# Expert blocks of 96 rows and twelve overflow blocks in a one-core mixture-of-experts decoder step

## What is computed

```python
logits = (xt @ w_router) + router_bias
probs = jax.nn.softmax(logits, axis=-1)
...                                   # best group of 4 experts, then the top 2 of that group
for e in range(N_EXPERTS):            # 16
    h = jax.nn.silu(xt @ w_gate[e]) * (xt @ w_up[e])      # 1024 -> 512
    y = y + gates[:, e:e + 1] * (h @ w_down[e])           # 512 -> 1024
```

## Time and profile before

| | us |
|---|---|
| median of 3 runs | 719.52 |
| lowest and highest | 718.69, 720.13 |
| the profiled execution: its time | 722.82 |
| its span in the trace | 721.0 |

### The profile page before, as it was taken

One profiled execution on the slowest core, in us unless ns is written; L12 is line 12 of the kernel. 1 busy time (PEld: TensorE's weight loads), 2 busy tenths in 40 slices (PEclk: granted clock), 3 DMA queues, 4 the chain that ended last, 5 costly groups with the idle time before them and its releaser, 6 DMA issues. The chain is left out here.

```text
span 721.0 us, 9573 instructions
## 1 busy us (share of the span) xinstructions
PE 663.5 (92%) x3807; PEld 556.4 (77%) x3807; DVE 508.0 (70%) x580; ACT 339.5 (47%) x334; POOL 125.4 (17%) x77
## 2 busy tenths in 40 slices
PE   6999999988999999999428899999999999999776
PEld 5999899988997886587417788888888888887431
DVE  4226447799575474776483899999999999998247
ACT  4437413322153421013305677777777777777100
POOL 0001323333033201200020011111111111100140
PEclk9999999999999999999559999999999999999896
DMA  9941212212512014097165799999999999990172
GB/s 285 383 167 60 78 40 88 89 59 79 156 60 76 1 49 152 21 357 271 60 223 242 283 378 410 412 415 403 408 416 411 400 410 415 410 384 37 62 275 95
DMA packets 48689, 162.56 MB, mean 225 GB/s; under 512 B 4294, under 2 KB 23450, under 8 KB 36364
## 3 DMA queue, kind: packets, MB, share of 16 engines
q1 hardware_dynamic: 41756, 136.62, 50.1%
q0 software_dynamic: 6896, 25.43, 9.0%
HBM read 142.61 MB, written 19.44 MB: 225 GB/s over the span
## 5 line engine op out<-in xcount | busy, mean ns | idle before, releaser
L1300 DVE TENSOR_TENSOR RA<-FA,RA 128x2048 fp32r<-128x2048 f32 x93 | 212.9, 2290 | 34.9 <-ACT RA L848 34.2
L848 ACT ACTIVATE RA<-FA 128x2048 fp32r<-128x2048 f32 x93 | 178.7, 1923 | 51.0 <-PE bank L1733 34.9
L1733 PE MATMUL bank<-RA 128*128 128x512 f32 x768 | 188.3, 401 | 3.7 <-DVE RA L1305 2.1
L1733 PEld LDWEIGHTS bank<-RA 128*128 128x128 f32 x768 | 143.9, 192 | 36.3 <-DVE RA L1305 2.7
L1479 PE MATMUL bank<-RA 128*128 128x272 f32 x432 | 110.4, 292 | 0.0
L1480 PE MATMUL bank<-RA 128*128 128x272 f32 x432 | 109.8, 290 | 0.0
L1745 PE MATMUL bank<-RA 128*128 128x512 f32 x384 | 91.3, 394 | 2.1 <-DVE RA L1310 2.1
L1745 PEld LDWEIGHTS bank<-RA 128*128 128x128 f32 x384 | 73.0, 190 | 17.5 <-DVE RA L1310 2.2
L1479 PEld LDWEIGHTS bank<-RA 128*128 128x128 f32 x432 | 82.5, 191 | 0.0
L1480 PEld LDWEIGHTS bank<-RA 128*128 128x128 f32 x432 | 82.5, 191 | 0.0
L969 DVE TENSOR_TENSOR RA<-FA,RA 128x2048 fp32r<-128x2048 f32 (+1 forms) x18 | 48.6, 2700 | 28.7 <-ACT RA L707 28.4
(11 more groups left out here) (223 smaller groups left out, 733.7 us busy)
## 6 DMA issues: line engine op xcount, KB each, us to landing
FA<-w_up SPq DMA_DIRECT2D x32, 1024.0 KB, 7.1
FA<-w_gate SPq DMA_DIRECT2D x32, 1024.0 KB, 6.8
FA<-w_down SPq DMA_DIRECT2D x32, 1024.0 KB, 7.6
FA<-w_in SPq DMA_DIRECT2D x13, 1024.0 KB, 5.1
y_by_slot<-FA POOLq DMA_DIRECT2D x16, 512.0 KB, 7.2
y_by_slot<-FA POOLq DMA_DIRECT2D x1, 4096.0 KB, 18.5
FA<-w_out SPq DMA_DIRECT2D x4, 1024.0 KB, 5.1
FA<-x_prompt SPq DMA_DIRECT2D x8, 256.0 KB, 5.5
```

Source lines behind the costliest of these rows:

```text
L848: nc.scalar.activation(split[split_slot(bi, j)][0], raw[place], ACT.Copy).then_inc(m_hi, 1)
L1300: tt_(sl[1], raw[place], f(sl[0]), ALU.subtract).then_inc(m_lo, 1)
L1733: last = mm(out[:, :], xgT[par][x_][:, kt, :], w[w_][:, t, :], start=(kt == 0 and i == 0), stop=(kt == KT - 1 and i == 2))
```

## The change

Blocks hold at most 96 rows (`CAP`), and there are twelve overflow blocks. Slots in DRAM stay 128 rows apart. All products, transposes, copies, gathers and stores of a block take 96 rows in place of 128; where the block's rows are partitions this shortens no instruction's free size, and where they lie along the free size it becomes 384 or 96 in place of 512 or 128. Since 96 is no power of two, DVE gets three instructions more in the routing chain, which count how often a rank passes a multiple of 96. A second fill writes zeros into rows 96 to 127 of the first 16 blocks. The fullest expert has 82 rows, so neither version runs an overflow block.

```diff
-NOV = 8
+NOV = 12
+CAP = 96
@@ routing on DVE
-            full = small[:, SM_BLK + 1:SM_BLK + NTT].unsqueeze(1).broadcast_to([P, E, 4])
-            link(tt_(more, cnt.unsqueeze(2).broadcast_to([P, E, 4]), full, ALU.is_gt))
+            limits = small[:, SM_CAP:SM_CAP + NCAP].unsqueeze(1)
+            link(tt_(more, cnt.unsqueeze(2).broadcast_to([P, E, NCAP]), limits.broadcast_to([P, E, NCAP]), ALU.is_gt))
...
             link(stt(tmp, before, -1.0, eo, ALU.add, ALU.add))
-            link(stt(t3(over), in_tile.rearrange("p (t e) -> p t e", t=NTT), float(P),
+            link(tt_(past, in_tile.unsqueeze(2).broadcast_to([P, NE, NCAP]), limits.broadcast_to([P, NE, NCAP]), ALU.is_ge))
+            link(nc.vector.tensor_reduce(pm, past, AX, ALU.add))
+            link(stt(base, pm, float(P - CAP), base, ALU.mult, ALU.add))
+            link(stt(t3(over), in_tile.rearrange("p (t e) -> p t e", t=NTT), float(CAP),
                      tmp.unsqueeze(1).broadcast_to([P, NTT, E]), ALU.is_ge, ALU.mult))
@@ one-hot rows
-                tt_(row_hot[:, sl], iota_h.unsqueeze(1).broadcast_to([P, NTT, P]),
-                    row[:, sl].unsqueeze(2).broadcast_to([P, NTT, P]), ALU.is_equal).then_inc(s_hot, 1)
+                tt_(row_hot[:, sl], iota_h[:, 0:CAP].unsqueeze(1).broadcast_to([P, NTT, CAP]),
+                    row[:, sl].unsqueeze(2).broadcast_to([P, NTT, CAP]), ALU.is_equal).then_inc(s_hot, 1)
@@ fill on POOL
             pool.dma_start(yg_dram[E * P:NBLK * P, :].rearrange("(b p) n -> p b n", p=P), fill_src).then_inc(s_fill, 16)
+            pool.dma_start(yg_dram[0:E * P, :].rearrange("(b p) n -> p b n", p=P)[CAP:P],
+                           fa(32 * K, D)[CAP:P].unsqueeze(1).broadcast_to([P - CAP, E, D])).then_inc(s_fill, 16)
@@ store on POOL
-                pool.dma_start(y_slot[bi], ysb[par]).then_inc(m_st[par], 16)
+                pool.dma_start(y_slot[bi][0:CAP], ysb[par][0:CAP]).then_inc(m_st[par], 16)
@@ low halves of a block's rows on DVE (the high halves on ACT alike)
-                    tt_(xgT[par][1][:, 4 * c:4 * c + 4, :], bank[c][:, :].rearrange("p (k t) -> p k t", k=4),
-                        f(xgT[par][0][:, 4 * c:4 * c + 4, :]), ALU.subtract).then_inc(m_tl, 1)
+                    tt_(xgT[par][1][:, 4 * c:4 * c + 4, 0:CAP], bank[c][:, 0:4 * CAP].rearrange("p (k t) -> p k t", k=4),
+                        f(xgT[par][0][:, 4 * c:4 * c + 4, 0:CAP]), ALU.subtract).then_inc(m_tl, 1)
@@ PE: the transposes of a block's rows, a gate or up product, a down product
-                        last = tr(bank[c][:, t * P:(t + 1) * P], xg[par][:, c * 512 + t:(c + 1) * 512:4], ident)
+                        last = tr(bank[c][:, t * CAP:(t + 1) * CAP], xg[par][0:CAP, c * 512 + t:(c + 1) * 512:4], ident[0:CAP, 0:CAP])
...
-                        last = mm(out[:, :], xgT[par][x_][:, kt, :], w[w_][:, t, :],
+                        last = mm(out[0:CAP, :], xgT[par][x_][:, kt, 0:CAP], w[w_][:, t, :],
...
-                            last = mm(bank[5 + g][:, :], hT[x_][:, kt, :], w[w_][:, t, 512 * g:512 * g + 512],
+                            last = mm(bank[5 + g][0:CAP, :], hT[x_][:, kt, 0:CAP], w[w_][:, t, 512 * g:512 * g + 512],
```

More of the change, by code:

```diff
@@ L197, in half @@
             return fa(off, n // 2).bitcast(BF16)
-        row_hot = half(B0, 2 * NTT * P).rearrange("p (s r) -> p s r", s=2 * NTT)
+        row_hot = half(B0, 2 * NTT * CAP).rearrange("p (s r) -> p s r", s=2 * NTT)
         off_blk = fa(B0 + 1024, 2 * NTT * NBLK).rearrange("p (s b) -> p s b", s=2 * NTT)
@@ L626, in gather @@
                 pool.indirect_dma_start(
-                    out=xg[par], out_offset=None, in_=x1_dram,
-                    in_offset=bass.IndirectOffsetOnAxis(ap=ids[:, bi:bi + 1].bitcast(U32), axis=0)).then_inc(m_xg[par], 16)
+                    out=xg[par][0:CAP], out_offset=None, in_=x1_dram,
+                    in_offset=bass.IndirectOffsetOnAxis(ap=ids[0:CAP, bi:bi + 1].bitcast(U32), axis=0)).then_inc(m_xg[par], 16)
             pool.wait_ge(s_x1s, 16 * NTT)
@@ L864, in silu @@
                     act.wait_ge(m_h, bi)
-                nc.scalar.activation(silu_g, bank[2][:, :], ACT.Silu).then_inc(m_sg, 1)
+                nc.scalar.activation(silu_g[0:CAP], bank[2][0:CAP, :], ACT.Silu).then_inc(m_sg, 1)
             def y_half(bi, par):
@@ L870, in y_half @@
                     act.wait_ge(m_st[par], store_count(bi, par))
-                nc.scalar.activation(ysb[par][:, 0:512], bank[5][:, :], ACT.Copy).then_inc(m_ya, 1)
+                nc.scalar.activation(ysb[par][0:CAP, 0:512], bank[5][0:CAP, :], ACT.Copy).then_inc(m_ya, 1)
             def step(bi, par, s=None, i=0):
@@ L1190, in _ @@
             base, nb, before, over = rb(360, NE), rb(440, 32), rb(472, E), rb(504, NE)
-            more = rb(664, 4 * E).rearrange("p (e j) -> p e j", e=E)
-            rank, tmp = rb(264, NE), rb(728, E)
+            more = rb(664, NCAP * E).rearrange("p (e j) -> p e j", e=E)
+            rank, tmp = rb(264, NE), rb(760, E)
+            past = fa(B0 + 1024, NE * NCAP).rearrange("p (x j) -> p x j", j=NCAP)
             prod = fa(B0 + 1024, 2 * NE)
@@ L1710, in _ @@
                     for w in range(2):
-                        last = mm(bank[5][:, 0:NBLK], row_hot[0:rows, i, :], in_blk[0:rows, i, w, :],
+                        last = mm(bank[5][0:CAP, 0:NBLK], row_hot[0:rows, i, :], in_blk[0:rows, i, w, :],
                                   start=(i == 0 and w == 0), stop=(i == 2 * NTT - 1 and w == 1))
@@ L1754, in h_turn @@
                     c, t = kt // 2, kt % 2
-                    last = tr(bank[4][:, kt * P:(kt + 1) * P], hbuf[:, c * 256 + t:(c + 1) * 256:2], ident)
+                    last = tr(bank[4][:, kt * CAP:(kt + 1) * CAP], hbuf[0:CAP, c * 256 + t:(c + 1) * 256:2], ident[0:CAP, 0:CAP])
                 last.then_inc(m_ht, 1)
```

26 lines of the change are left out of this document (14 added, 12 removed).

## The result

| | before | after |
|---|---|---|
| median (4 runs each) | 719.83 us | 731.14 us |
| ratio | | 1.0129, 95% interval 1.0099 to 1.0159 |
| the profiled execution's span | 721.0 | 730.9 |

The change makes the kernel 1.3% slower, about 9 us, by the ratio with its interval. (The two medians of four lie further apart, 11.3 us.) Repeated beside other runs of the kernel before (median 722.4), it was 1.0095 (1.0063 to 1.0126), about 7 us. The forecast was 721.1 with a range of 716.0 to 723.3: the sign was right, and the size was far off.

What follows compares the result with a forecast made beforehand. PE, nine tenths busy or more in nearly every slice, was taken as the bound. Terms +1.3 + 1.05 - 0.27 - 0.1 (steady stretch) - 0.35 = +1.6 us gave 721.1; range 716.0 to 723.3, the forecast's own 719.2 to 722.9.

Steps and rivals of the forecast that it cites:

- Routing, +1.3 us: Serial DVE chain until `ids`: three new steps and more blocks, less shorter one-hot rows, +1.3 us, between +0.9 and +1.9.
- The table, +1.05: Overflow table on DVE: four more pairs take 1.65 us, 0.6 of it covered; exposed +1.05 us, between 0.6 and 1.65.
- `x_lo`, -0.27: Low half before the first product, for which PE waits: two instructions go from 1.29 to 1.02 us, -0.27.
- A: Rival, faster: the moving identity sets the transposes' pace, so narrowing it saves 5.2 us, giving 715.9; chance 0.13.
- B: Rival, no difference: transposes lose their stride penalty, or table and chain end low with 1 us from the clock; 719.1; chance 0.25.
- C: Rival, slower: the second fill from 32 partitions runs slowly and delays the `w_in` piece; 721.5 to 730; chance 0.06.
- D: Rival: an expert with more than 96 rows would run an overflow block of 17.9 us; fullest has 82, so none.
- Products, 0: Expert products on PE: 96 instead of 128 stationary columns buys nothing, 0, bounded by -0.3 us.
- transposes, 0: Transposes on PE: the stationary side of 128 strided columns sets 0.120 us a step and is unchanged, so 0.
- the transposes' half of B: Transposes on PE lose only their penalty for the stride, 0.012 us each over 172, 2.1 us.
- The tail, -0.35: After the last expert: shorter `h_lo` and a smaller last store before the final gathers, -0.35 us, between 0 and -0.8.
- The fill, 0: Second fill adds 10.5 us ahead of the `w_in` piece, landing at about 48, before ACT's use at 52.94: hidden, 0.

Runs made afterwards that it cites:

- after_cast_128: The changed kernel with one edit: DVE copies the index list on 128 partitions again instead of 96; 725.55 us, ratio 1.0044 to the kernel before.
- after_tokens_128: The changed kernel with one-hot rows and index products back at 128 columns and the index copy on 128 partitions; ratio 1.0026 to the kernel before.

## Why the prediction was wrong

The direction has a reason and isn't luck: without the slow gather the changed kernel is still slower, by the two terms of the sum that were positive. The size failed, by one wait. The working, step by step:

- **Routing, +1.3 us: +1.84.** The DVE terms were right. 1.33 and the 0.53 us of the second ten index products give 1.86. The missing term is PE's, which stood nowhere in my list: I had taken a narrower stationary operand as free, from products of 512 moving columns, and these have 28. The copy itself comes 2.79 us later; 0.95 of that stands ahead of the chain.
- **The table, +1.05, and `x_lo`, -0.27: the step that failed.** "The gather and the transposes move with `ids`, so the cover stays." The gather did not move with `ids`: it came 6.6 us late, 4.4 on POOL and 2.2 that go with the weights issued ahead, and the first product came 5.8 us later after the copy, not 0.8. The wait had been taken as fixed; it grew from one low half to three. Where the copy is on 128 partitions, in after_cast_128 and after_tokens_128, the distance is 13.6 and 13.7 us against 12.8 to 13.0, +0.6 to +0.9: there the sum of the two terms, +0.78, holds. The time, too, by and large: 1.0044 and 1.0026, +3.2 and +1.9 us, where the sum said +1.6 and with PE's term 2.1.
- **The warning** stood in the trace of the kernel before: its first two gathers, beside the low halves, take 2.26 and 1.82 us and its third 0.94 (the rows above). Had I asked what they waited for, a longer wait would have been a rival. None of A, B, C and D held it.
- **Products, 0, and transposes, 0: right.** 288.1 us from first to last gate product in both; eight transposes 1.10 us after 1.12, so rival A and the transposes' half of B are out. The four of the hidden rows end 0.10 us sooner (0.60 after 0.70), and 24 down products take 0.07 more (5.68 after 5.61), which cancel. The prediction's "whatever the stride" is my reading of the Trainium skill ("TensorE: Matmul & The Clock Gate", the section on LDWEIGHTS), whose formula names the columns alone; no row here bears it out, and strided transposes follow each other at 0.120 us where contiguous ones do at 0.108.
- **The tail, -0.35: right in part.** From the last store to the first of the final gathers it is 5.03 us, before 5.21, -0.18; over all profiles it is 4.97 to 5.04 with stores of 96 rows and 5.02 to 5.33 with 128. The span after the start of the last gate product is 1.3 us longer in the first profile of after (56.9) than in the first of before (55.6), but 57.0 and 57.1 in the second ones, so the change has no share in it. What it goes with is PE's granted clock: in both kernels it is 54.9 to 55.8 us where the clock falls to 0.50 for 3.4 us at a time three times between 664 and 701 us, and 56.6 to 57.3 where it falls for 6.8 us twice.
- **The fill, 0: the result right, the picture wrong.** The `w_in` piece before the fill landed at 38.0 us, as before (37.7), and not at 48. The one behind was hit, landing at 55.9 in place of 43.2, 22.6 us after issue, and ACT used it at 64.5, so 8.6 us were left. Rival C didn't come.
- **The range of the sum was added up wrong.** With every bound given and the clock at their ends the terms make -1.2 to +4.3 us, so 718.4 to 723.8, not 719.2 to 722.9. The measured 731.1 lies outside both.

The sum had no term for a wait that was already there, whose length hangs on a border between two instructions. The two first profiles differ by 9.9 us: 0.95 ahead of the chain, 1.84 of routing, 5.8 of the gather (with the table in its shadow) and 1.3 behind the last gate product. The two second ones differ by 8.0: 0.8, 1.8, 5.4 and nothing. So 7.2 to 7.7 us belong to the change; that the 0.8 to 0.95 us ahead of the chain do too isn't shown.

## What to carry to other kernels

When an instruction on POOL takes two or three times as long in one place as in others, as the gathers do here (2.26 and 0.94 us), ask what it waits for, and put a rival beside the sum in which that wait grows to the whole run of long instructions next to it. Issue the gather for which PE waits beside short DVE instructions; one that ran beside `x_lo`, which reads PSUM, took 0.94 us. And the cut from 128 to 96 rows saved nothing in products with 512 moving columns (5.68 us for 24 after 5.61), while short bf16 products got slower.

## What the runs showed of the hardware

- A gather issued by POOL takes 0.90 to 1.03 us where no low half runs, and up to 6.7 beside three low halves of 2.28 us on DVE; it ends 0.8 to 0.9 us after one of them. For all gathers but the slow first ones that is the low half during which they start.
- Which one it is for the first gather goes with the copy that writes its index list: 2.2 to 2.4 us in seven profiles where the copy that POOL waits for covers partitions 96 to 127, 6.6 to 6.7 in eight where it doesn't. The cause is open.
- bf16 products of 24 to 28 moving columns follow each other at 0.027 us with 128 stationary columns and at 0.080 with 96.
